# The first norm of a two-block transformer kernel: five of eight parts of its modulation summed by TensorE, and the bias tables between the first two pairs

## What is computed

```python
def rms_norm(x, g):
    y = x * rsqrt(mean(x * x, axis=-1) + EPS)
    return y * g

def adaln_pre(h, g, shift, scale):
    return rms_norm(h, g) * (1 + scale) + shift

def swiglu(h, w13, w2):
    a, b = split(h @ w13, 2)
    return (silu(a) * b) @ w2

cond = silu(c)
mod = (cond @ ada_w[l] + ada_b[l]).reshape(3 sublayers, 3, D)
h = adaln_pre(x, norm_g[l, 0], mod[0, 0], mod[0, 1])
x = x + 0.5 * mod[0, 2] * swiglu(h, ffn1_w13[l], ffn1_w2[l])
```

## Time and profile before

| | |
|---|---|
| median of three runs | 3389.28 us (3389.25 to 3390.62) |
| profiled execution | 3389.15 us |
| its span, first to last instruction | 3387.4 us |
| mean granted clock of TensorE | 0.997 of full speed |
| TensorE busy | 3329.7 us, 98% of the span, 19808 matmuls |
| VectorE busy | 2267.5 us, 67% |
| ScalarE busy | 1317.6 us, 39% |
| GpSimd busy | 438.0 us, 13% |
| DMA | 380.9 MB, mean 112 GB/s |

### The profile page before, as it was taken

The page is one execution under the profiler, slowest core; times in us unless marked ns, Lnnn a source line. Parts: engine busy times, 40 slices in busy tenths (PEclk is TensorE's granted clock), DMA queues, the critical chain, the costliest instruction groups (busy, mean ns, idle before and its releaser), DMA issues. The chain is left out here.

```text
span 3387.4 us, 51035 instructions
## 1 busy us (share of the span) xinstructions
PE 3329.7 (98%) x19808; PEld 2811.7 (83%) x19808; DVE 2267.5 (67%) x3615; ACT 1317.6 (39%) x2095; POOL 438.0 (13%) x329
## 2 busy tenths in 40 slices
PE   8999999999999999999999999999999999999999
PEld 7989877788888898987778888886888888788887
DVE  6877757658775677785765877657666525766642
ACT  5424344535333433334453523243443324443321
POOL 2000200222000300020022200121200011120002
PEclk9999999999999999999999999999999999999999
DMA  6463523113542345442201353321233332223332
GB/s 252 148 229 129 166 86 94 32 39 127 176 145 96 112 154 211 144 150 88 87 26 54 128 192 124 101 77 52 81 99 99 105 102 63 68 82 94 96 104 85
DMA packets 88629, 380.90 MB, mean 112 GB/s; under 512 B 9774, under 2 KB 10926, under 8 KB 77192
## 3 DMA queue, kind: packets, MB, share of 16 engines
q1 hardware_dynamic: 88456, 378.52, 33.5%
HBM read 376.36 MB, written 2.12 MB: 112 GB/s over the span
## 5 line engine op out<-in xcount | busy, mean ns | idle before, releaser
L2001 DVE TENSOR_TENSOR wL<-wR,wH 128x1024 fp32r<-128x1024 f32 (+2 forms) x160 | 207.9, 1299 | 195.4 <-ACT wH L1289 195.2
L1289 ACT ACTIVATE wH<-wR 128x1024 fp32r<-128x1024 f32 (+2 forms) x158 | 175.0, 1107 | 381.3 <-PE bank L3452 305.6
L3697 PE MATMUL bank<-hH,wH 128*128 128x512 f32 x640 | 271.6, 424 | 0.0
L3566 PE MATMUL bank<-gHc,wH 128*128 128x512 f32 x660 | 256.8, 389 | 0.0
L3567 PE MATMUL bank<-gHc,wL 128*128 128x512 f32 x660 | 256.8, 389 | 0.0
L3568 PE MATMUL bank<-gLc,wH 128*128 128x512 f32 x660 | 256.7, 389 | 0.0
L3699 PE MATMUL bank<-hL,wH 128*128 128x512 f32 x640 | 251.6, 393 | 0.0
L3539 PE MATMUL bank<-hH,wH 128*128 128x512 f32 x640 | 249.7, 390 | 1.2 <-DVE wL L2057 1.2
L3698 PE MATMUL bank<-hH,wL 128*128 128x512 f32 x640 | 250.5, 391 | 0.0
L3540 PE MATMUL bank<-hH,wL 128*128 128x512 f32 x640 | 249.4, 390 | 0.0
L3541 PE MATMUL bank<-hL,wH 128*128 128x512 f32 x640 | 249.0, 389 | 0.0
(11 more groups left out here) (567 smaller groups left out, 8683.0 us busy)
## 6 DMA issues: line engine op xcount, KB each, us to landing
RW<-in_ffn_wq SPq DMA_DIRECT2D x80, 1024.0 KB, 5.6
adaw<-in_ada_w SPq DMA_DIRECT2D x144, 512.0 KB, 4.4
wR<-in_w_up SPq DMA_DIRECT2D x88, 512.0 KB, 3.6
wR<-in_ffn_w SPq DMA_DIRECT2D x56, 704.0 KB, 4.1
wR<-in_w_mix SPq DMA_DIRECT2D x72, 512.0 KB, 3.6
wR<-in_w_down SPq DMA_DIRECT2D x32, 704.0 KB, 4.1
wR<-in_w_in SPq DMA_DIRECT2D x40, 512.0 KB, 3.6
ada<-in_ada_first SPq DMA_DIRECT2D x8, 1024.0 KB, 12.1
```

Source lines behind the costliest of these rows:

```text
L3566: pe.matmul(o, wh[:, k, :], gHc[:, k, c], start=k == 0, stop=False)
L3697: pe.matmul(o, wH[n][:, k, :], hH[:, k, :], start=k == 0, stop=False)
```

## The change

- **Parts 0 to 4 by TensorE.** The host lays parts 0 to 4 of `ada_first` out by column (condition features on the partitions) and leaves parts 5 to 7 by row. TensorE turns the condition (eight small transposes; ScalarE copies them to `CT`), and `part_sums` multiplies a part by it: eight products with 32 output columns and 256 moving columns, in two rounds that write four strips of 32 rows of one bank. ScalarE copies the bank to `DS`; `part_columns` adds the four strips and turns the sums into two columns by two products with `picks`, a column with four ones that GpSimd writes at the start. VectorE adds the biases (`shifted`) and forms `modA` of one tile (`scaled_by`). Parts 5 to 7 are still VectorE's `dots`, which now stand between the tiles.
- **Copies and squares.** The copies of x from the banks are shared: even tiles VectorE, odd tiles ScalarE. Squares stay in eight buffers, VectorE adds them up in seven steps, and one product with ones of 512 columns takes the place of sixteen of 256. A table load for logarithm and exponential stands in front on ScalarE. The `warm` products are gone.
- **Four units tile by tile.** `first_four` takes the place of `open_three` and `products_third` in layer 0: for each tile the products of units 0 and 1 (whole 512 columns, L3679 to L3681 of the new kernel) as soon as both halves of `hL` are there; from tile 2 on those of unit 2, and from tile 4 on those of unit 3, whose weights stand in `fourth`. Between tiles stand the columns and sums of later parts, and behind tile 2's the five bias rows.
- **Bias tables.** The four products of `bias_tables` move from before unit 3 to between `classical(f, 0)` and `classical(f, 1, 0, 6)`. On ScalarE the four copies to `bm` stand behind what the first pair and part of the second need, and ahead of the rest.
- **Loads.** SyncE issues the biases and gains first, then parts 0 to 4 with units 0 and 1, then units 2 and 3 between parts 5 to 7, with new waits: parts 5 and 6 on columns already made (they take the buffers of parts 0 and 1), part 7 on the last transposes, and pair 0 on the columns of part 3.

```diff
-ADA_PARTS = tuple((2 * c, 2 * c + 2) for c in range(KT))
+FIRST_TILES = (26, 30, 34, 38, 8, 12)
+FIRST_PE = 5
...
+        first_rows = [place(f"ada0{t}", [P, 2, D], at=o_g + t * TB) for t in FIRST_TILES]
+        ada0 = [first_rows[c] for c in (0, 1, 2, 3, 4, 0, 1, 5)]
...
                 if c >= 4:
                     sp.wait_ge(S.ada0_in[c % 4], 16)
+                if c in (5, 6):
+                    sp.wait_ge(S.dc, c - 4)
+                if c == 7:
+                    sp.wait_ge(S.x_turned, KT)
...
+                    sp.wait_ge(S.dc, 4)
+                    pair(f, 0, wq, l)
                     sp.wait_ge(S.bias_sb, 1)
...
+                    pair(f, 1, wq, l)
                     sp.wait_ge(S.bias_out, 32)
+                    sp.wait_ge(S.dc, 5)
+                    sp.wait_ge(S.ada0_done, 2)
...
                 if between:
+                    gate_silu(0, 0)
+                    group1(f, 0)
+                    pair_high(0)
+                    gate_silu(1, 2)
+                    act.wait_ge(S.w_used, at(S.w_used, ubase + 4))
+                    single(f, 0, 2, 2)
+                    single(f, 0, 3, 5)
+                    pair_high(1)
+                    sum_high(f, sub, 0)
                     between()
...
+                first_high(0)
+                first_sums(0)
+                first_high(1)
+                first_sums(1)
+                act.wait_ge(S.ms, 1)
+                act.activation(rstd[:, :], bank[MS_BANK[0]][:, :], ACT.Ln, bias=eps, scale=1.0 / D).then_inc(S.ln, 2)
...
+                first_sums(2)
+                for k in range(KT):
+                    for e, c in enumerate(HALVES):
+                        act.wait_ge(S.hf, 2 * k + e + 1)
+                        act.activation(hH[:, k, c], HB[e][k // TT][:, k % TT, :], ACT.Identity,
+                                       bias=mod[:, k:k + 1]).then_inc(S.h_hi, 1)
+                    if k == 0:
+                        first_sums(3)
+                        first_high(2)
+                    if k == 1:
+                        first_sums(4)
+                    if k == 2:
+                        first_high(3, fourth)
+                    if k == 3:
+                        first_bias()
...
+                low(0)
+                part(0)
+                low(1)
+                part(1)
+                normed(0)
+                normed(1)
+                for k in range(KT):
+                    normed_low(k)
+                    if k + 2 < KT:
+                        part(k + 2)
+                        normed(k + 2)
+                    if k in (1, 3):
+                        low(2 + k // 2)
...
+            part_sums(0)
+            pe.wait_ge(S.sq_sum, KT - 1)
+            pe.matmul(bank[MS_BANK[0]][:, :], ones, squares[0], start=True, stop=True).then_inc(S.ms, 2)
+            part_columns(0)
+            part_sums(1)
+            part_columns(1)
+            part_sums(2)
...
+                for k in range(KT):
+                    pe.wait_ge(S.h_lo, 2 * k + 2)
+                    for u in range(2):
+                        part(u, k)
+                    if k < 3:
+                        part_columns(k + 2)
+                    if k < 2:
+                        part_sums(k + 3)
+                    if k == 2:
+                        bias_rows()
+                        pe.wait_ge(S.w_lo, 3)
+                        for r in range(2):
+                            part(2, r)
+                    if k >= 2:
+                        part(2, k)
...
                     classical(f, 0)
+                    if between:
+                        between()
                     classical(f, 1, 0, 6)
...
-                if l == 0:
-                    warm(24)
-                    pe.wait_ge(S.mod_set, at(S.mod_set, 2))
-                    warm(3)
```

The new functions that these lines call, with the sums and the columns of a part on TensorE:

```diff
+                for r in range(2):
+                    for g in range(4):
+                        mm = pe.matmul(bank[DS_BANK[c % 2]][32 * g:32 * (g + 1), 0:2 * P], CT[:, 4 * r + g, :], rows[:, 4 * r + g, :],
+                                       start=r == 0, stop=r == 1)
...
+                for j in range(2):
+                    mm = pe.matmul(bank[DC_BANK[c % 2]][:, j:j + 1], DS[c % 2][:, j * P:(j + 1) * P], picks[:, :], start=True, stop=True)
```

More of the change, by code:

```diff
@@ L2166, in chunk, with ffn @@
                 g_low(f, q1)
-            def ffn(f, sub, n, ubase, udn, gates, ahead, part, rest=None):
+            def ffn(f, sub, n, ubase, udn, gates, ahead, part, rest=None, start=False):
                 def pair_out(i, b):
@@ L3569, in rows, with chunk @@
                 return mm
-            def chunk(f, u, half, xdone, xbase, ss=None):
+            def chunk(f, u, half, xdone, xbase, ss=None, between=None):
                 if half:
```

328 lines of the change are left out of this document (221 added, 107 removed).

## The result

The changed kernel took 3413.11 us (median of four runs, 3412.07 to 3414.12) where the kernel before took 3389.95 beside it; the ratio is 1.0068, with a 95% interval of 1.005 to 1.0085. The direction was forecast, the size was not: 23.2 us slower instead of 11.5, and 3.1 us above the top of the range. The profiled execution took 3414.12 us, 25.0 above that of before.

What follows compares the result with a forecast made beforehand. TensorE, busy 98% of the span, was taken as the bound; second pair +10.4 us (first pair +0.5, then the wait for moved bias tables) plus 1.1 for clock gave +11.5, 3400.7 us; range 3392 to 3410.

Steps and rivals of the forecast that it cites:

- The first product: Start of tile 0 on TensorE: at 33.0 us instead of 44.1, 11.1 us earlier.
- the root: First norm on ScalarE: logarithm and exponential for the inverse root, behind the copy of part 1's sums, done at 30.3 us.
- Four sums at once: Sums of a part on TensorE: four 32-column products run together, 0.9 us at full clock, twice that at half.
- ScalarE's order between tiles 0 and 1: Copy of sums and a unit's high part precede tile 1's: 6.0 us a tile, TensorE idling 2.9.
- a stall behind the bias products: Ahead of the second pair: TensorE waits 6.3 us for ScalarE's copies and high parts, then VectorE's weights.
- the first pair later than before: End of the tile stage: first pair at 71.0 us, 0.5 later than in the kernel before.
- What held the start at 44 us is VectorE.: Kernel before, first tiles: eight parts of the first modulation, two dot products of 1.23 us each, delay TensorE's first product.
- I let it be half from 20.8 to 28 again.: TensorE's clock at the start: half rate only from 20.8 to 28 us, as in the earlier trace.
- VectorE's tile 6: Late tile stage: VectorE's dots and steps finish tile 6 at 64.0 us, then ten pieces of 0.69 remain.
- rival 1: Tile stage: pauses keep the clock half to 40 or 46 us; +14.8 to +16.4 at second pair, about 3406; chance 0.18.
- GpSimd's 32 copies and block differences end near 84, under the bias products.: Between the first two pairs: GpSimd's work is done near 84 us and costs nothing.
- the clock behind the stall: From the second pair on: possible half clock after 6.3 us of idleness, taken as 1.1 us between 0 and 2.1.

Runs made afterwards that it cites:

- e3: The changed kernel with ScalarE's four bias-table copies behind the second pair's high parts instead of ahead of them; 3410.59 us, ratio 1.0061.
- b1: The kernel before with only its bias tables moved between the first two pairs and ScalarE's copies moved behind the first pair's work; 3401.07 us, ratio 1.0039.
- e10: The kernel before, unchanged, profiled a second time to look at its early clock; 3389.09 us.
- e1: The changed kernel with 23 unread constant products filling TensorE's waits between the transposes and tile 2; 3404.54 us, ratio 1.0044.
- e11: The changed kernel, unchanged, profiled a second time to look at its clock; 3411.49 us.
- e2: The changed kernel with GpSimd's four raw-weight sums held until VectorE has made the second pair's low parts; 3409.30 us, ratio 1.0060.
- e5: The changed kernel with GpSimd's block differences ahead of its 32 copies, its sums held back and ScalarE's table copies later; 3406.15 us, ratio 1.0053.
- e9: The changed kernel with all mends combined and skewed tables loaded earlier, bias tables still between the first two pairs; 3392.56 us, ratio 1.0009.
- e4: The changed kernel with sums and columns one tile earlier on TensorE and tile 1's high part ahead of a unit's; 3403.62 us, ratio 1.0042.
- e6: The changed kernel with sums and columns one tile earlier, plus ten constant products in TensorE's waits up to tile 0; 3397.16 us, ratio 1.0028.
- e7: The changed kernel with tile stage and second pair's chain mended, bias rows at the start, seven parts on TensorE, GpSimd's copies first; 3389.82 us, ratio 1.0007.
- e8: The changed kernel with all mends combined, skewed tables loaded earlier, bias tables ahead of unit 3's last tiles, GpSimd's block differences held; 3387.76 us, ratio 0.9998.

## Why the prediction was wrong in size

**What held.** The first product (33.0 forecast, 32.52 measured), in part by luck: the root was there at 29.0 instead of 30.3 (the terms written down for it give 29.8), and then tile 0's high part waited on ScalarE for the copy of part 2's sums, which starts at 30.68 and which the sum does not have. Four sums at once (0.9 forecast, 1.17 measured with the tail of the last); ScalarE's order between tiles 0 and 1 as the cause of a pause; a stall behind the bias products, ended by VectorE's weights, of whose causes the place of ScalarE's copies is one (e3, b1); the first pair later than before in spite of the early start.

**A reading that was wrong and cost nothing: "What held the start at 44 us is VectorE."** VectorE's first low part was done at 39.8, while TensorE was busy with its constants without a gap from 32.64 to 44.46, late behind squares at half clock. In e10, at full clock, those constants did wait for VectorE, until 39.54.

**The step that failed first: "I let it be half from 20.8 to 28 again."** The clock was half until 45 and from 49 to 63 us. First pair: 71.0 forecast, 77.35 measured, 6.35 missed. In e1, at full clock until 47.9, it stands at 67.70, and there VectorE's tile 6 sets the pace as forecast: TensorE waits for it until 60.61, where the sum had 64.0. Of the 3.3 us between 71.0 and 67.70, 2.1 are the half clock to 28 that the sum did count (first product at 30.88 in e1 instead of 33.0), and 1.2 are steps that it had too long. So the clock cost 9.65 us in this execution, 7.55 more than was counted, and set the pace instead of VectorE: TensorE worked without a wait from 50.85 to 77.35.

This is rival 1, and larger than its own price of 4.4 to 6.0 at the second pair (+14.8 to +16.4 instead of +10.4), since I let the clock recover by 46 and it fell again at 49. In the second execution (e11) 3.3 us were missed at the first pair instead of 6.35. I had written against it that "each pause follows 3 us of full work"; that work ran at half clock and did not bring the clock back in time. The Trainium skill (TensorE: Matmul & The Clock Gate, Why this matters for your kernels) warns of pauses between bursts, though of longer ones than these. The traces go the same way: pauses of 1.9, 2.8 and 1.8 us between tiles with the clock at half, and with constants in the waits of e1 the clock at 1 until 47.9.

**The step that failed second: "GpSimd's 32 copies and block differences end near 84, under the bias products."** The first three block differences ended at 89.3, the last at 94.4 and the sums at 100. The sum took VectorE's 1.6, 1.14 and 1.22 us from the earlier trace rows, where GpSimd was idle; beside GpSimd the first two took 4.71 and 2.28, 4.2 us more, and the third, behind GpSimd's end, its usual time. Idle stretch: 6.3 forecast, 10.35 measured, 4.05 missed, and e2 gave back 4.1. The trace of before had the warning, in VectorE's low part of a unit of 128x1024, beside GpSimd's block differences:

```profile
59.67 2.95 DVE L2237 TENSOR_TENSOR wL<-wR,wH 128x1024 fp32r<-128x1024 f32 x1 [5.50 <-ACT wH L1308]
```

A step of the same shape takes 1.22 in the earlier trace rows. The Trainium skill (SBUF — State Buffer, Who interferes with whom) says that a VectorE instruction with two inputs in SBUF contends with a GpSimd instruction that reads SBUF. The traces agree, with 0.42 us a piece alone and 1.48 beside GpSimd's sums.

**The step that was mis-sized: the clock behind the stall.** I took 1.1 us between 0 and 2.1; it was 2.3.

The three account for the difference: 6.35 + 4.05 + 1.2 = 11.6, and 11.5 + 11.6 = 23.1 us against 23.2 measured. That it meets the medians so closely is luck, since the share of the clock changes from execution to execution: in e11 the block products stand 2.5 us earlier. The tables' place was weighed too lightly all the same: I priced its wait at 6.3 us inside a sum, and b1 shows that alone it costs 12.2, of which the half clock behind it has 1.8 (12.63 us from the second pair to the block products instead of 10.88).

## What to carry to other kernels

A pause of TensorE may have to be counted twice, once for itself and once for the products that run at half clock behind it; the constants of e1, which fill such pauses, were worth 7.5 us of the median. When a duration is taken from a row, look at what GpSimd does beside it, there and in the new place; a chain that alternates ScalarE, VectorE and GpSimd must be moved as a whole, since taking away its latest link shows the next (e3, e5, e9). Work that could run at another time, such as these tables, is dear just ahead of a step whose operands other engines make only behind it (b1: 12.2 us).

## What the runs showed of the hardware that was not expected

- The clock of the same stretch differs between executions of the same program: the kernel before at half around 24 us in one profile and at full in another, with the first product 2.8 us apart, and 3389.15 and 3389.09 us in all. Of the 2.8 us, 0.6 were left at the block products (92.24 and 91.62), so an early gain of some microseconds in the first tiles need not reach the end.
- The clock can fall in a pause or behind it. It fell in the 10.35 us of the change, at 96.7, and in the 2.76 us ahead of tile 1 in e2, e3, e5 and e11, some 0.5 to 0.75 us before their end; in the change at 48.9 and in e4 at 42.7 it fell about a microsecond after full products had begun again. A pause does not always bring a fall: the same 1.58 us ahead of tile 2 did in e4 and did not in e6, the same 1.86 ahead of the block products did in e5 and did not in e9. And thin products are no sure cover: in e1 it fell at 47.9 us with 3 us of bias rows (33 rows by 4 columns) just behind it and no pause, while in e6 it stayed at 1 through the same rows.
- Between GpSimd and VectorE the loser depends on the instructions. Beside GpSimd's block differences and sums a piece of VectorE takes about as long as one of theirs. In e7 it is GpSimd's last block difference that takes 5.11 us instead of 2.35, while four steps of VectorE beside it keep their usual times (a fifth takes 2.82 instead of 1.21). GpSimd's 32 small copies leave VectorE's steps at their usual times and are slowed themselves: 4.80 us with VectorE almost idle (e8), 7.77 in the change, 12.40 beside steady work (e5).
- Falls of the clock far behind the changed code come and go as well, and e8's lead went into one. The same instruction of ScalarE starts at 554.33 us in the profile of the kernel before and at 550.85 in that of e8, and another at 591.32 and 590.40: 3.5 us of lead became 0.9. In between e8 ran at half clock (one stretch of its table), which the kernel before did not in that profile and did for a shorter time in e10:

```profile
568.00:570.00 2.00, 2.00 (x9) 1.67 (x8) 1.60 (x7) 0.38 (x1) 0.00 (x0) 0.50 0.00 0
```

This is one execution; whether it accounts for the 1.5 us of the median was not shown.
